# Output projections of two of eight units by seven products on token halves, with weight sums made by DMA in between

## What is computed

```python
for i in range(DEPTH):                      # DEPTH = 2
    proj = h @ w_in[i]
    ...                                     # y_conv, y_swa, y_ret, y_rwkv
    mix = jnp.concatenate([y_conv, y_swa, y_ret, y_rwkv], axis=-1) @ w_out[i]
    h = layer_norm(ALPHA * h + mix, ln1_g[i], ln1_b[i])
    h = layer_norm(ALPHA * h + conv_glu_ffn(h, ffn_w_up[i], ffn_conv_w[i], ffn_w_down[i]), ln2_g[i], ln2_b[i])
```

## Time and profile before

| | us |
|---|---|
| median of 3 runs | 3052.5 (3052.41 to 3058.36) |
| the profiled execution, its own time | 3056.32 |
| its span, first to last instruction | 3054.4 |
| PE busy | 3011.8 (99%) |
| PEld busy | 2759.9 (90%) |
| DVE busy | 1529.4 (50%) |
| ACT busy | 939.6 (31%) |
| POOL busy | 216.8 (7%) |

### The profile page before, as it was taken

One profiled execution on the slowest core, in us unless ns is written; L12 is line 12 of the kernel. 1 busy time (PEld: TensorE's weight loads), 2 busy tenths in 40 slices (PEclk: granted clock), 3 DMA queues, 4 the chain that ended last, 5 costly groups with the idle time before them and its releaser, 6 DMA issues.

```text
span 3054.4 us, 64343 instructions
## 1 busy us (share of the span) xinstructions
PE 3011.8 (99%) x27180; PEld 2759.9 (90%) x27180; DVE 1529.4 (50%) x3672; ACT 939.6 (31%) x2381; POOL 216.8 (7%) x319
## 2 busy tenths in 40 slices
PE   8999999999999999999999999999999999999998
PEld 7788778889898899989989899999999999999998
DVE  4345552355633455336554366544566255663562
ACT  3324440134421343124341144303343043421320
POOL 0111010011101110010010101000000000000000
PEclk9999999999999999999999999999999999999999
DMA  7577477788978989888797898986768857787887
GB/s 256 170 205 213 118 208 218 220 237 283 311 236 263 280 273 320 242 259 272 238 313 210 264 276 261 295 284 196 260 205 268 290 178 249 210 267 253 301 302 248
DMA packets 227116, 760.19 MB, mean 249 GB/s; under 512 B 25088, under 2 KB 44672, under 8 KB 226576
## 3 DMA queue, kind: packets, MB, share of 16 engines
q1 hardware_dynamic: 189328, 620.80, 61.6%
q0 software_dynamic: 37504, 135.28, 18.0%
HBM read 744.33 MB, written 136.31 MB: 288 GB/s over the span
## 4 chain that ended last, share of the span: by engine, by line
PE 92%; DMA 3%; DVE 3%; ACT 2%; issue 0%; SPq 0%; ACTq 0%; DVEq 0%
PE psum L1853 29%; PE psum L1306 27%; PE psum L1876 10%; PE psum L1912 8%; PE psum L1443 7%; DMA slots<-in_weights 2%; PE psum L1300 1%; PE psum L1322 1%; PE psum L1621 1%; PE psum L1646 1%; DMA slots<-wsum 1%; PE psum L1633 1%; PE psum L1572 1%; PE psum L1694 1%; PE psum L1803 1%
## 5 line engine op out<-in xcount | busy, mean ns | idle before, releaser
L1306 PE MATMUL psum<-hT,slots 128*128 128x256 f32 (+1 forms) x2880 | 658.9, 387 | 2.8 <-ACT hT L874 2.1
L1306 PEld LDWEIGHTS psum<-hT,slots 128*128 128x128 f32 x2880 | 541.6, 190 | 97.0 <-issue 5.5
L1853 PE MATMUL psum<-tsum,slots 128*128 128x128 f32 (+1 forms) x4928 | 608.0, 277 | 11.6 <-ACT raw L1223 4.9
L1853 PEld LDWEIGHTS psum<-tsum,slots 128*128 128x128 f32 x4928 | 573.1, 191 | 28.6 <-issue 20.2
L1853 PE MATMUL psum<-hT,slots 128*128 128x128 f32 (+1 forms) x3696 | 453.7, 276 | 6.9 <-DMA slots<-in_weights 3.9
L1853 PEld LDWEIGHTS psum<-hT,slots 128*128 128x128 f32 x3696 | 432.6, 192 | 10.1 <-DMA slots<-in_weights 4.9
L1876 PE MATMUL psum<-gT,slots 128*128 128x256 f32 (+1 forms) x1408 | 309.9, 383 | 0.0
L1876 PEld LDWEIGHTS psum<-gT,slots 128*128 128x128 f32 x1408 | 267.1, 190 | 40.9
L1306 PE MATMUL psum<-mixT,slots 128*128 128x256 f32 (+2 forms) x1024 | 226.4, 381 | 1.1 <-DVE hT L2030 1.1
L1306 PEld LDWEIGHTS psum<-mixT,slots 128*128 128x128 f32 x1024 | 194.3, 190 | 29.7 <-issue 1.5
L2030 DVE SCALAR_TENSOR_TENSOR hT<-hT,psum 128x256 f32<-128x256 f32 (+2 forms) x96 | 40.5, 423 | 348.3 <-PE psum L1876 249.7
(11 more groups left out here) (326 smaller groups left out, 3526.6 us busy)
## 6 DMA issues: line engine op xcount, KB each, us to landing
slots<-in_weights SPq DMA_DIRECT2D x667, 512.0 KB, 4.6
slots<-wsum SPq DMA_DIRECT2D x308, 512.0 KB, 4.5
wsum<-in_weights POOLq DMA_DIRECT2D x132, 512.0 KB, 6.7
slots<-wsumi SPq DMA_DIRECT2D x64, 512.0 KB, 4.4
slots<-wsumd SPq DMA_DIRECT2D x64, 512.0 KB, 4.5
wsum<-wsum POOLq DMA_DIRECT2D x44, 512.0 KB, 7.9
wsumi<-in_weights POOLq DMA_DIRECT2D x24, 512.0 KB, 7.5
wsumd<-in_weights POOLq DMA_DIRECT2D x24, 512.0 KB, 9.3
```

The source lines that it names most:

```text
L1306: ins = mm(psum[:, i % 2, :n], lhsT, rhs, start=k == 0, stop=k == len(pairs) - 1)
L1853: ins = mm(dst[:, e * n:(e + 1) * n], w[:, (4 * e + k) * P:(4 * e + k + 1) * P], moving[s][k], start=s in (0, 1, 5) and e == 0 and k == 0, ...
```

## The change

Units 5 and 6 (`OUT_FAST`) get their output projection by seven products for each half of the output features: 14 products `os{g}_{s}` of eight matmuls with 128 columns, each from one slot of weights, in place of eight blocks of eight matmuls with 256 columns. The quarters' layout in HBM is changed, so that in the other six units two slots hold the weights of two output blocks together. The weight sums lie in `wsumo`. They are made by a new generator `out_sums` on POOL: eight copies of 512 KB and eight adding DMAs, of which the first four wait for all eight copies, the next two for those four, and the last two for these. Its 16 points lie in the down projection of unit 2 and in the first seven input blocks of unit 4. POOL's program calls it at `u == 3`, behind `sums_until(1, first_up)` and ahead of `rwkv(4)`. The token sums are made on DVE (`mix_sums`, four operations) in the down projection of the unit before, into `tsum`, which the up projection uses too. The residual steps on DVE are 14 in place of eight, and the steps of the owed norm come one a product from the third product on, the rest of them behind the last product. The four semaphores of `down_sums` become one (`wd_made`), with the same order of waits.

```diff
+OUT_FAST = [5, 6]
...
+def out_spare():
+
+    return [i for i, (u, name) in enumerate(BLOCKS) if (u == 2 and name[:2] in ("dn", "ds")) or (u == NCH and name in MIX_PART)]
...
-            out.append((l, N_IN + int(name[3:]), u, name, None))
+            m = int(name[3:])
+            if m % 2 == 0:
+                out += [(l, N_IN + m + half, u, f"out{m + 1}", None) for half in range(2)]
+        elif name[:2] == "os":
+            g, s = map(int, name[2:].split("_"))
+            kind = STEPS7[s]
+            which = (g, SUMS.index(kind)) if kind[0] == "S" else N_IN + 4 * g + QUADS.index(kind)
+            out.append((l, which, u, name, None))
...
+                elif name[:2] == "os":
+                    if name == "os0_1" and u == OUT_FAST[0]:
+                        sp.wait_ge(S["wo_made"], 256)
+                    source = weights[l, which] if STEPS7[int(name[-1])][0] == "A" else wsumo[which]
...
-                for kind, more, ready, count, done in (("S1", "A22", "wd_copy", 384, "wd_first"), ("S3", "A21", "wd_copy", 384, "wd_first"),
-                                                       ("S2", "S1", "wd_first", 192, "wd_second"), ("S4", "S2", "wd_second", 96, "wd_third")):
+                                        max_dma_last_dim=4096).then_inc(S["wd_made"], 16)
+                for kind, more, count in (("S1", "A22", 384), ("S3", "A21", 384), ("S2", "S1", 576), ("S4", "S2", 672)):
                     for group in range(2):
                         for b in range(DN_BLOCKS):
                             yield in_time()
-                            g.wait_ge(S[ready], count)
+                            g.wait_ge(S["wd_made"], count)
...
+            def out_sums():
+                steps, at = out_spare(), 0
+
+                def in_time():
+                    nonlocal at
+                    at += 1
+                    return steps[len(steps) * (at - 1) // 16]
+
+                for group in range(2):
+                    for kind, first in (("S1", "A21"), ("S3", "A11"), ("S2", "A11"), ("S4", "A12")):
+                        yield in_time()
+                        g.dma_start(out_block(kind, group), out_block(first, group), max_dma_last_dim=4096).then_inc(S["wo_made"], 16)
+                for kind, more, count in (("S1", "A22", 128), ("S3", "A21", 128), ("S2", "S1", 192), ("S4", "S2", 224)):
+                    for group in range(2):
+                        yield in_time()
+                        g.wait_ge(S["wo_made"], count)
+                        g.dma_start(out_block(kind, group), out_block(more, group), accum_op=ALU.add,
+                                    max_dma_last_dim=4096).then_inc(S["wo_made"], 16)
+
+            sums += [down_sums(), input_sums(), out_sums()]
+            pending += [next(sums[k]) for k in range(2, 5)]
...
                 if 1 < u <= NCH:
                     sums_until(1, first_up)
+                if u == NCH - 1:
+                    sums_until(4, first_up)
...
                 pe.wait_ge(S["a_mix"], tiles_before(u) + nt)
-                for m in range(KD):
-                    rest(dense(u, f"out{m}", [mixT[:, k, first:n] for k in range(KD)]))
-                    if 0 < u < NU - 1 and m == 0:
-                        ln_mean(2 * u - 1)
-                    if 0 < u < NU - 1 and m == 4:
-                        ln_var(2 * u - 1)
+                if u in OUT_FAST:
+                    out_by_seven(u, [mixT[:, k, first:n] for k in range(KD)])
+                    return
+                for m in range(0, KD, 2):
+                    w = [next_slot(), next_slot()]
+                    for e in range(2):
+                        rest(feature(u, f"out{m + e}", [(w[k // 4][:, 512 * e + k % 4 * P:512 * e + (k % 4 + 1) * P],
+                                                         mixT[:, k, first:n]) for k in range(KD)]))
+                        if 0 < u < NU - 1 and m + e == 0:
+                            ln_mean(2 * u - 1)
+                        if 0 < u < NU - 1 and m + e == 4:
+                            ln_var(2 * u - 1)
...
+            def out_by_seven(u, x):
+
+                n = span_of(u, 0)[1] // 2
+                old, new = [y[:, 0:n] for y in x], [y[:, n:2 * n] for y in x]
+                t1, t3, t2, t4 = ([tsum[:, j, k, :n] for k in range(4)] for j in range(4))
+                moving = [old[:4], t1, t2, new[4:], t3, old[4:], t4]
+                for g in range(2):
+                    base = AT[u, f"os{g}_0"]
+                    for s in range(7):
+                        w = next_slot()
+                        bank_free(base + s)
+                        if (g, s) == (0, 1):
+                            pe.wait_ge(S["osum"], 4 * (OUT_FAST.index(u) + 1))
+                        dst = product_at(u, base, s)
+                        for e in range(2):
+                            for k in range(4):
+                                ins = mm(dst[:, e * n:(e + 1) * n], w[:, (4 * e + k) * P:(4 * e + k + 1) * P], moving[s][k],
+                                         start=s in (0, 1, 5) and e == 0 and k == 0, stop=k == 3, skip_group_check=True)
+                        ins.then_inc(S["blk"], 1)
+                        if (g, s) == (0, 1):
+                            ln_mean(2 * u - 1)
+                        if (g, s) == (1, 5):
+                            ln_var(2 * u - 1)
 
             def up(u):
...
+            def mix_sums(u):
+
+                first, n = span_of(u, 0)[0] - chunk_of(u)[0], span_of(u, 0)[1]
+                h, before = n // 2, 4 * OUT_FAST.index(u)
+                b11, b12 = (mixT[:, 0:4, first + h * i:first + h * (i + 1)] for i in range(2))
+                b21, b22 = (mixT[:, 4:8, first + h * i:first + h * (i + 1)] for i in range(2))
+                t1, t3, t2, t4 = (tsum[:, j, :, :h] for j in range(4))
+                v.wait_ge(S["conv"], 2 * u + 2)
+                v.wait_ge(S["w_mix"], 2 * u + 2)
+                v.wait_ge(S["r_mix"], u + 1)
+                v.wait_ge(S["a_mix"], tiles_before(u) + len(tiles_of(u)))
+                v.wait_ge(S["blk"], AT[u - 1, up_names(u - 1)[-1]] + 1)
+                tt(t1, b11, b12, ALU.subtract).then_inc(S["osum"], 1)
+                tt(t3, b22, b12, ALU.subtract).then_inc(S["osum"], 1)
+                v.wait_ge(S["osum"], before + 2)
+                stt(t2, t3, -1.0, b11, ALU.mult, ALU.subtract).then_inc(S["osum"], 1)
+                v.wait_ge(S["osum"], before + 3)
+                stt(t4, t2, -1.0, b21, ALU.mult, ALU.subtract).then_inc(S["osum"], 1)
+
+            def out_step(u, g, s):
...
                 program = later_norm(2 * u - 1) if 0 < u < NU - 1 else iter(())
+                if u in OUT_FAST:
+                    for g in range(2):
+                        for s in range(7):
+                            out_step(u, g, s)
+                            if g or s > 1:
+                                advance(program, 1)
+                    rest(program)
+                    return
                 for m in range(KD):
...
                             residual_by_seven(u, g, s)
+                            if u + 1 in OUT_FAST and (g, s) == (1, 4):
+                                mix_sums(u + 1)
```

More of the change, by code:

```diff
@@ L71, in down_names, with out_names @@
     return [f"ds{g}_{s}" for g in range(2) for s in range(7)] if u in DN_FAST else [f"dn{m}" for m in range(KD)]
+def out_names(u):
+    return [f"os{g}_{s}" for g in range(2) for s in range(7)] if u in OUT_FAST else [f"out{m}" for m in range(KD)]
 def down_yields(u):
@@ L89, in width @@
 def width(u, name):
-    if name[:3] == "out" or name[:2] == "up":
+    if name[:2] in ("ou", "up"):
         return span_of(u, 0)[1]
@@ L176, in all_blocks @@
     for u in range(NU - 1):
-        out += [(u, f"out{m}") for m in range(KD)]
+        out += [(u, name) for name in out_names(u)]
         out += [(u + 1, name) for name in in_order(u + 1)]
@@ L180, in all_blocks @@
         if u == NU - 2:
-            out += [(u + 1, f"out{m}") for m in range(KD)]
+            out += [(u + 1, name) for name in out_names(u + 1)]
         out += [(u, name) for name in down_names(u)]
@@ L211, in sum_points @@
             kind = name[:2]
-            if l == 0 and u == 0 and v == 0 and (name in IN_TILES or kind == "ou"):
+            if l == 0 and u == 0 and v == 0 and (name in IN_TILES or kind in ("ou", "os")):
                 spare.append(i)
@@ L219, in sum_points @@
                 spare.append(i)
-            if (l or u == 0) and v == u + 1 and kind == "ou":
+            if (l or u == 0) and v == u + 1 and kind in ("ou", "os"):
                 spare.append(i)
@@ L239, in by_vector @@
 def by_vector(name):
-    return name[:3] == "out" or name[:2] in ("dn", "ds")
+    return name[:2] in ("ou", "os", "dn", "ds")
 MEAN_BANK, VAR_BANK = 5, 4
@@ L410, in build @@
         wsumi = nc.dram_tensor("wsumi", (len(IN_GROUPS), 4, P, 1024), F32, kind="Internal").ap()
+        wsumo = nc.dram_tensor("wsumo", (2, 4, P, 1024), F32, kind="Internal").ap()
```

(16 more changed lines are left out.)

26 lines of the change are left out of this document (15 added, 11 removed).

## The result

The changed kernel takes 3087.99 us (median of 4 runs, 3084.68 to 3090.72) against 3054.94 us of the kernel before in 4 runs (3052.41 to 3058.36): 33 us slower, a ratio of 1.0107 with a 95% interval of 1.0091 to 1.0123. The forecast was 3080, with a range of 3067 to 3096. Part of the 8 us between the two is the reference: the forecast stood on 3052.5 for the kernel before, which is 3054.94 over all its runs.

What follows compares the result with a forecast made beforehand. The prediction took PE, busy 99% of the span, as the bound. Products -5.2, stall +30.6 and clock +2 gave +27.4 us on a median of 3052.5, so 3080 us, with a range of 3067 to 3096.

Steps and rivals of the forecast that it cites:

- The mechanism: POOL issues its sixteen DMAs as a burst ahead of unit 4's mask operations, and PE waits for those masks.
- The stall: PE's wait for unit 4's masks, going on at about 1498.7 in place of 1468.05: 30.6 us, likely 20 to 43.
- the first adds: The burst's first four adding DMAs, behind the copies: about 14 us, landed at 1487.
- The products: Fourteen smaller products in the output projections of units 5 and 6: 2.6 us gained in each, 5.2 us together.
- The clock: PE's lowered clock after the one long stall: 2 us lost.
- the sum of 3101: Forecast total in us if the clock's loss grew with idle time, to 23 us in place of 2.
- Loads during the copies: Weight loads beside POOL's copies, 1446 to 1469 us: taken to add 0, bounded at 3 us.
- The late norm: Owed norm's tail behind the output projection's last step, delaying the next input projection: taken as 0, bounded at 3 us a unit.
- A, POOL in time: Rival: POOL is through before PE needs the masks, only the products count; 3047 us, chance 0.04.
- B, a short stall: Rival: the burst has the DMA engines nearly alone, stall of 7 to 18 us; 3056 to 3067 us, chance 0.08.
- C, a long one: Rival: adding DMAs land slowly in both stages, or the clock's loss grows with the stall; 3096 to 3115 us, chance 0.07.
- D, no burst if the sums are spread: Rival: sums spread over unit 2's down projection, as their points say, POOL idle there; 3047 us, chance 0.01.

Runs made afterwards that it cites:

- e3: The changed kernel with POOL making the sixteen sums behind the mask operations for unit 4's mixer instead of ahead of them; 3052.58 us, ratio 0.9991 to the kernel before.
- e4: The changed kernel with the eight copies still ahead of the mask operations and the eight adding DMAs behind them; 3055.88 us, ratio 0.9998 to the kernel before.
- e8: The changed kernel with eight copies and the first four adding DMAs ahead of the masks, the last four adds behind; 3075.09 us, ratio 1.0060 to the kernel before.
- e6: The changed kernel with the sixteen sums merged by their points with the up projection's sums, still ahead of the masks; 3064.01 us, ratio 1.0023 to the kernel before.
- e2: The changed kernel with no output projection by seven products, POOL still making the sixteen sums, which nothing reads; 3090.46 us, ratio 1.0117 to the kernel before.
- e5: e3 with the owed norm finished inside the two output projections by seven; 3052.20 us, ratio 0.9988 to the kernel before.
- e9: e5 with the sixteen sums as one burst behind POOL's last sum for the down projection, at about 1953 us; 3065.67 us, ratio 1.0032 to the kernel before.
- e10: e5 with unit 4's output projection by seven products as well; 3067.95 us, ratio 1.0036 to the kernel before.
- e7: e5 with the sixteen sums spread over unit 3's down projection and unit 4's output projection; 3068.81 us, ratio 1.0037 to the kernel before.

## Why the prediction was right, and which terms were off

**The mechanism** was the forecast's: POOL's program stands for the sixteen DMAs, and PE waits for the masks behind them. e3, e4 and e8 show it by taking it away, and by the dose.

**The stall**, 30.6 us forecast, was 31.1 as a wait, but that closeness is in part luck. The forecast counted from a PE that comes to its wait undelayed, and PE came 2.8 us late. From its undelayed arrival the stall is 33.9, 3.3 us more than forecast. POOL's chain has these 3 us: copies landed 28.4 us after the first issue (27.3 forecast), the first adds took 17.1 (14), the next 8.4 (9). The first adds are the term that was low. POOL's own row shows a cause: the fourth adding DMA was issued 8.46 us after the third ended, "issue" by name, when the first three had landed and the DMA engines stood idle (the last numbers: clock, DMA share, GB/s):

```profile
1488.00:1490.00 2.00, 0.00 (x0) 0.00 (x0) 0.00 (x0) 0.00 (x0) 0.81 (x1) 0.50 0.00 0
```

**The products**, -5.2: measured -2.6 and -2.6 (37.8 to 35.3 and 36.3 to 33.7 in the ledger).

**The clock**, 2 us: from the first waiting matmul to L1681 it is 1505.55 to 1513.47, 7.9 us, for what took 1468.05 to 1473.14 before, 5.1 us: 2.8. Half clock (1.2 GHz) was granted for about 6 us after 31 us of idle time, against 4 after 2.2 us. The loss was 1.7 us after 2.2 us of idle time, 2.8 after 6.9 (e6), 2.8 after 16.6 (e8), and 2.8 and 2.1 after 31 (the changed kernel and e2). It did not go with the idle time, so the sum of 3101 is out. The Trainium skill's account in "TensorE: Matmul & The Clock Gate", section "What's actually happening", two levels that follow recent activity, agrees.

**Loads during the copies** were taken as 0 with a bound of 3: they made PE 2.8 us later. From the start that the ledger has to the end of the last product ahead of the wait (its start and the 1.88 us it takes to the next start) it is 1449.82 to 1474.29, before 1446.34 to 1468.05. In the changed kernel these 2.8 us cost nothing of their own: PE waits for POOL behind them, and would have waited 33.9 us in place of 31.1, as the prediction said of a late PE. Where PE doesn't wait for POOL they are on the path: e4's PE is 3.0 us later there than e3's, of the 3.3 between the two. I had set 0 because the burst from 1533 to 1567 held up nothing. The 86% in the earlier trace rows was the better row: there the loads want 62% of the engines.

**The late norm** was taken as 0 with a bound of 3 a unit: the ledger has 1.0 and 1.5 us. The step that failed left an engine out. I followed the norm's tail on VectorE only. It did end where I put it (the copy 6.0 us into the input projection), but ScalarE has its eight affine steps to do behind it, ahead of the first block's eviction:

```profile
2145.86 2.77 DVE L2217 TENSOR_TENSOR hT<-hT,rstdT 128x256 f32<-128x256 f32 x8
2148.55 0.17 DVE L2254 COPY rows<-last 128x7 f32<-128x7 f32 x1
```

```profile
2146.32 4.04 ACT L947 ACTIVATE hT<-hT,par 128x256 f32<-128x256 f32 x8 [4.88 <-DVE hT L2217]
2150.27 0.14 ACT L974 ACTIVATE last<-psum 128x1 f32<-128x1 f32 x1
2150.32 0.36 ACT L975 ACTIVATE rows<-psum 128x256 f32<-128x256 f32 x1
```

```profile
2150.82 7.14 PE L1354 MATMUL psum<-hT,slots 128*128 128x256 f32 x32 [0.77 <-ACT rows L975]
```

PE's third block waits 0.77 us for that eviction, in unit 7's input projection 0.8 us too. e5 shows that the norm was the cause: with its steps inside the projection both waits and both losses are gone. Where the ledger's rest beside the waits lies (0.2 and 0.7 us) was not followed up, but for 0.5 us of waits for a load in unit 7.

**The rest.** Of the 34.5 us between the two profiles, -5.2 + 33.9 + 2.8 + 2.5 are 34.0. The 0.5 left over is a balance of larger things: 3.5 us ahead of unit 3's up projection and 1.2 in unit 5's input projection, against -2.9 in the rest of unit 3's up projection, -0.9 in unit 4's and -0.6 in unit 6's up projection. I take them for loads that landed otherwise, as the other kernels show them too, in both directions; that is not shown. The profiles are 7.1 us further apart than the forecast's +27.4 and the medians 5.6. The terms that were low are the stall (3.3), the late norm (2.5) and the clock (0.8).

**The rivals.** A, POOL in time, B, a short stall, and C, a long one, fell: the wait is 31.1 us. D, no burst if the sums are spread, was priced at A's time, 3047. e6_as_meant spreads them by their points and takes 3064: at least in that form the price of the rival was wrong, as POOL stands for the new DMAs there too and PE waits for loads.

## What to carry to other kernels

When work is added to an in-order engine, read what stands behind it in that engine's order, not the point that the code names for it: a point that has passed is a burst, and an adding DMA that waits for its copies makes the engine stand. Put such a chain behind what others wait for, and then price its traffic by what the loads beside it want of the DMA engines: here it was free at 48%, and cost 3 us (eight copies alone) at 62% and 13 us at 69%. Fewer multiplications in exchange for nearly twice the loads is a gain only where the DMA engines have that room.

## What the runs showed of the hardware that was not expected

Adding DMAs that POOL issues from HBM to HBM did not always go out freely. Of each burst's first four into `wsumo`, three went out back to back, and the fourth only 8.1 to 14.0 us after them, with no semaphore that the profile shows. That is so in all eight kernels that have them in a row (8.06 us in e2, 8.46 in the changed kernel, 8.71 in e8, 11.44 in e3, 12.93 in e9, 13.06 in e5, 13.49 in e4, 13.96 in e10). Adding DMAs don't always show it: the kernel before issued six for `wsumd` in a row in 5.04 us. And copies can show it too: thirteen went out in one go before, but as four and nine in e5, e8 and e10, where they stand right behind the new sums, with 8.8 to 10.0 us between; in e9 there are 4.95 us after six. What limits them was not tried.

Spreading the sixteen DMAs did not make them cheap: they cost nothing measurable as one burst at 1533, 14 us in the stage behind them when spread over units 2 and 4 (e6), and 16 us spread over units 3 and 4 (e7). In both kernels POOL stood for its own DMAs and then issued the late ones together, so whether an even spread would cost anything is not shown.
